# Latent layers of a PEER transformer, reworked as one stage each, in blocks of 128 tokens

## The reference

```python
for i in range(DEPTH):                     # 2
    h  = modulate(rms_norm_2(x, norm1_gain[i]), sh1, sc1)
    hc = modulate(rms_norm_2(xc, norm1_gain[i]), csh1, csc1)
    q, k, v = project_qkv(h, w_qkv[i], ..., rope)      # 8 heads, 2 kv heads, head width 128
    qc, kc, vc = project_qkv(hc, w_qkv[i], ..., None)
    o = latent attention over context and latent keys  # i = 0: global; i = 1: a window and a sink
    x = x + g1 * (o @ w_o[i])
    if not last: xc = xc + cg1 * (context_attention(...) @ w_o[i])
    h2 = modulate(rms_norm_2(x, norm2_gain[i]), sh2, sc2)
    x = x + g2 * peer_ffn(h2, ...)
    if not last: xc = xc + cg2 * peer_ffn(h2c, ...)
```

## Time and profile before

| | us |
|---|---|
| runs | 3165.12, 3167.58, 3170.16 |
| median | 3167.58 |
| span of the profiled execution | 3163.4 |
| context's layer 0 (stages up to) | 284 |
| first block, layer 0 and layer 1 end at | 860 and 1428 |
| latent layer 0: attention, experts begin at | 1489, 1648 |
| latent layer 1: begins, attention, experts begin at | 2293, 2372, 2524 |
| `write_out` begins at | 3158.8 |
| busy: TensorE, VectorE, GpSimd, ScalarE | 2598.7, 2245.3, 1215.8, 584.7 |

### The profile page before, as it was taken

How to read it: one execution, slowest core, us unless ns; L and a number is a source line. 1 busy time by engine, 2 the same in 40 slices (tenths; PEclk the granted TensorE clock), 3 DMA queues, 4 the chain that set the end, 5 groups by cost and what they waited for, 6 DMA issues and landing times.

```text
span 3163.4 us, 30793 instructions
## 1 busy us (share of the span) xinstructions
PE 2598.7 (82%) x10048; PEld 1719.6 (54%) x10048; DVE 2245.3 (71%) x5446; ACT 584.7 (18%) x1613; POOL 1215.8 (38%) x1028
## 2 busy tenths in 40 slices
PE   6798786899797679998898787777799987877776
PEld 2677664788675568886683332332367733333222
DVE  0438978699788877768778886665563698866555
ACT  2221212100021120002321111121214211111111
POOL 0002543466564355651434444444200254444441
PEclk8899898999898899999999999999999999999999
DMA  9327876799998489994779999999731599999997
GB/s 391 148 95 250 323 277 226 274 386 390 374 347 317 170 303 380 409 409 163 240 263 420 420 420 420 420 420 420 314 109 54 232 419 420 420 420 420 420 420 290
DMA packets 209521, 1029.22 MB, mean 325 GB/s; under 512 B 23409, under 2 KB 24945, under 8 KB 142929
## 3 DMA queue, kind: packets, MB, share of 16 engines
q0 software_dynamic: 147456, 805.37, 63.9%
q1 hardware_dynamic: 60624, 217.34, 18.2%
q10 hardware_dynamic: 1280, 4.54, 0.4%
HBM read 1021.98 MB, written 5.18 MB: 325 GB/s over the span
## 4 chain that ended last, share of the span: by engine, by line
DMA 35%; PE 35%; DVE 22%; issue 4%; ACT 1%; POOL 1%; SPq 1%; DVEq 0%; ACTq 0%; another core or an unknown queue 0%; POOLq 0%
DMA w_ring<-in_peer_uv,expert 11%; PE ps L2410 6%; DMA own<-in_peer_uv,expert 6%; DMA ctx_ring<-in_peer_uv,expert 5%; PE ps L2060 5%; DVE sum L1442 4%; PE ps L449 4%; PE ps L1172 4%; PE ps L1253 3%; DMA w_ring<-in_weights 3%; PE ps L1759 3%; DMA ctx_ring<-in_peer_v,ctx_expert 3%; DMA hT<-in_peer_uv,expert 2%; DMA low<-in_peer_uv,expert 2%; DVE ctx_ring L1445 1%
## 5 line engine op out<-in xcount | busy, mean ns | idle before, releaser
L2410 PE MATMUL ps<-w_ring,diag 128*128 128x512 f32 x876 | 425.6, 631 | 120.6 <-ACT diag L2355 120.6
L2410 PEld LDWEIGHTS ps<-w_ring,diag 128*128 128x128 f32 x876 | 167.2, 199 | 374.6 <-ACT diag L2355 194.6
L2197 DVE SCALAR_TENSOR_TENSOR w_ring<-w_ring,htok 128x1024 f32<-128x1024 f32 x219 | 267.7, 1223 | 138.9 <-DMA w_ring<-in_peer_uv,expert 137.7
L2249 POOL DMA_INDIRECT w_ring<-in_peer_uv,expert x219 | 240.7, 1099 | 312.7 <-PE ps L2410 269.2
L1253 PE MATMUL ps<-mix,w_ring 128*128 128x256 f32 x1408 | 307.5, 382 | 8.8 <-DVE mix L395 8.8
L1425 POOL DMA_INDIRECT ctx_ring<-in_peer_u,ctx_expert x126 | 160.1, 1270 | 399.3 <-DVEq L1992 247.8
L1253 PEld LDWEIGHTS ps<-mix,w_ring 128*128 128x128 f32 x1408 | 269.6, 192 | 46.7 <-issue 9.6
L2355 ACT ACTIVATE diag<-consts_sb 128x128 f32<-128x128 f32 x512 | 179.0, 394 | 614.2 <-DVE consts_sb L2290 592.8
L1425 POOL DMA_INDIRECT ctx_ring<-in_peer_v,ctx_expert x152 | 187.8, 1235 | 230.2 <-DVE sum L1442 144.8
L2249 POOL DMA_INDIRECT own<-in_peer_uv,expert x75 | 83.8, 1117 | 346.2 <-DVEq L1992 260.9
L2410 PE MATMUL ps<-ctx_ring,diag 128*128 128x512 f32 x296 | 142.8, 618 | 41.2 <-ACT diag L2355 41.2
(11 more groups left out here) (437 smaller groups left out, 5027.6 us busy)
## 6 DMA issues: line engine op xcount, KB each, us to landing
w_ring<-in_weights SPq DMA_DIRECT2D x392, 512.0 KB
w_ring<-in_peer_uv,expert POOLq DMA_INDIRECT x219, 24.4
ctx_ring<-in_peer_v,ctx_expert POOLq DMA_INDIRECT x152
ctx_ring<-in_peer_u,ctx_expert POOLq DMA_INDIRECT x126
ctx_more<-in_peer_v,ctx_expert POOLq DMA_INDIRECT x104
consts_sb<-in_consts SPq DMA_DIRECT2D x1, 1536.0 KB, 9.8
ctx_more<-in_peer_u,ctx_expert POOLq DMA_INDIRECT x80
own<-in_peer_uv,expert POOLq DMA_INDIRECT x75
```

What stands on the lines that cost most here:

```text
L2197: v.scalar_tensor_tensor(out=u, in0=u, scalar=1.0, in1=m.htok[:, e // SLOTS, :], op0=ALU.mult, op1=ALU.mult, accum_out=m.dots[:, e:e + 1]) ...
L2249: pool.indirect_dma_start(out=entry(e), out_offset=None, in_=table, in_offset=bass.IndirectOffsetOnAxis(ap=m.expert[:, blk, k:k + 1], axis ...
L2410: ins = pe.matmul(m.ps[:, 2 * blk + half, :], b.diag[:, e % DIAGS, :], entry(e)[:, D + half * 512:D + (half + 1) * 512], start=(k == 0), s ...
```

## The change

Each latent layer becomes one stage (`latent_layer`), and its work goes by blocks of 128 tokens with tokens on the partitions:

- Products have 128 tokens as the stationary operand and 512 columns of weights as the moving one. An item is the keys and values of a block, or 4 heads' queries of a block. Layer 0 makes 6 items before attention; layer 1 makes 3, since its context's keys and block 0's keys and queries are made at the end of layer 0. Head norms are squares by ScalarE summed along the row, a root and a reciprocal a few elements wide. The gains of the heads are multiplied into the rotation's tables (`make_tables`).
- The stream stays by token (`m.x`). Its gates are needed as rows, so the gates of a layer are written to DRAM (`keep_gates`, in the context's projection and in the middle of layer 0) and read back to all partitions.
- The order is: attention of block 0, its output product, norm, queries of its first pair, routing steps 0 to 3; then attention of block 1 with steps 4 to 7 behind its first four heads. GpSimd starts the gathers there. Everything else stands between entries (`beside(e)` on TensorE, ScalarE and VectorE): the output product of block 1, the queries of the 7 other pairs of both blocks and their routings, in the order `SEQUENCE`, and in layer 0 the context's stream and the next layer's first items.
- Entry places: in layer 0, 4 own, 2 of the context's ring and the old stream's, 7 in all, and an eighth from entry 120; in layer 1 these 8 from the start, 2 more from entry 12 and 6 of the weight ring from entries 72, 88 and 104. A place taken again waits for `s.used` of its last entry.
- In layer 0 the weight groups of `peer_w_q` 1 to 3 and of the next layer's first items are loaded while entries run.
- The shares of the context rows change: in the first layer 30, 50, 24, 16, 106 (before 30, 48, 22, 16, 110), in the second 36, 50, 21, 17, 127 (before 114 in the last, `feed_forward`), in latent layer 0 35 (before 48). In that layer 3 rows stand behind each item and 2 behind each head of block 0.
- The output is written by token and in parts at the end of layer 1; the stage `write_out` is gone.

`project_qkv`, `second_attention` and `peer_queries` remain for the context alone, as `project_context`, `context_attention` and `context_queries`; `peer_experts` and `Entries` are gone.

```diff
-STAGE_SEMS = 46
+STAGE_SEMS = 56
...
-WEIGH_AT = (3, 1)
+WEIGH_AT = (2, 1)
...
-                    rows.take(v, 4 if j < WEIGH_AT[l] else 3 + j % 2, "feed_forward")
+                    rows.take(v, 4, "feed_forward")
...
-    FIRST_SHARE = dict(in_projection=30, rwkv=48, attention=22, out_projection=16, feed_forward=110)
-    SECOND_SHARE = dict(in_projection=36, rwkv=50, attention=21, out_projection=17, feed_forward=114)
-    TAIL_SHARE = dict(project_qkv=8, attention=16, out_projection=14, peer_queries=10)
+    FIRST_SHARE = dict(in_projection=30, rwkv=50, attention=24, out_projection=16, feed_forward=106)
+    SECOND_SHARE = dict(in_projection=36, rwkv=50, attention=21, out_projection=17, feed_forward=127)
+    TAIL_SHARE = dict(latent=35)
...
+def keep_gates(sp, m, i, kept):
+
+    for n, part in enumerate((G1, G2)):
+        sp.dma_start(m.kept_gates[i, n].rearrange("(k p) -> p k", p=P), m.mods[:, i, part:part + KT, LATENTS],
+                     allow_slow_non_contiguous=True).then_inc(kept, 16)
+    sp.wait_ge(kept, 32)
...
+SEQUENCE = ((0, 0), (0, 1), (0, 2), (1, 0), (0, 3), (1, 1), (1, 2), (1, 3))
+QUERY_AT = {1: 4, 2: 14, 3: 28, 4: 42, 5: 58, 6: 74, 7: 90}
+ROUTE_AT = {1: (14, 1), 2: (24, 2), 3: (44, 2), 4: (64, 2), 5: (84, 3), 6: (111, 3), 7: (145, 3)}
+X1_AT = 3
+MODS_AT, SUMS_AT, CONTEXT_AT = 106, 108, 116
+HTOK_AT = 124
+X0_AT = 130
+NEXT_AT = 140
...
+        opened = {f"own{j}": (0, None) for j in range(OWN)}
+        if i:
+            opened.update(ring0=(0, None), ring1=(0, None), stream=(0, None), sums=(0, None),
+                          keys=(12, (s.o_done, 2 * PAIRS)), queries=(12, wide.filled(("out", 1, 1))))
+            for j in range(1, NG_PQ):
+                slot = ring.slot_of[g0 + G_PQ + j]
+                for half in range(2):
+                    opened[f"group{2 * slot + half}"] = (QUERY_AT[PLACE_OF[1, j]] + 14, wide.filled(("pq", 1, j)))
+        else:
+            opened.update(ring0=(0, (m.ctx_used, TT * 2 * SLOTS)), ring1=(0, (m.ctx_used, TT * 2 * SLOTS)),
+                          stream=(0, turned.filled(("x", 1, 1))),
+                          sums=(SUMS_AT + 12, turned.filled(("sums", KT // 2 - 1))))
...
         @block.gpsimd
         def _(pool):
+            pool.wait_ge(m.joined, JOINING * m.stages)
             for e in range(TOTAL):
                 blk, k = e // SLOTS, e % SLOTS
                 if k % PAIR_SLOTS == 0:
-                    pool.wait_ge(m.routed, routed_count(1 + i, blk, k // PAIR_SLOTS))
...
+                    pool.wait_ge(m.routed, len(SEQUENCE) * (1 + i) + PLACE_OF[blk, k // PAIR_SLOTS] + 1)
+                if entries.before[e]:
+                    sem, count = entries.before[e]
+                    pool.wait_ge(s.used if sem is None else sem, count)
                 pool.indirect_dma_start(out=entry(e), out_offset=None, in_=table,
...
+            attend(0, None if i else lambda h: rows.take(v, 2, "latent"))
...
+            for half in range(2):
+                add_out(0, half)
+            norm_rows(("h2", 0))
+            norm_first_half(("h2", 0))
+            for at in range(4):
+                route_step(0, at)
+
+            def first_route(h):
+                if h < 4:
+                    route_step(0, 4 + h)
+                if h == 4:
+                    routes[0].shift(0, PAIR)
+            attend(1, first_route)
...
+                for n, (start, every) in ROUTE_AT.items():
+                    at = e - start
+                    if at >= 0 and at % every == 0 and at // every < Route.STEPS:
+                        route_step(n, at // every)
...
+                for n, at in QUERY_AT.items():
+                    if at <= e < at + 4:
...
+                        query_part(n, 2 * (e - at), 2 * (e - at) + 2)
```

More of the change, by code:

```diff
@@ L1522, in final_gain @@
     return m.vectors[:, FINAL_AT + k:FINAL_AT + k + 1]
-def write_out(nc, m, d):
-    with stage(m, "written") as (block, s, b):
-        @block.sync
-        def _(sp):
-            sp.dma_start(d.out, m.xT[:, :, :]).then_inc(s.written, 16)
-            sp.wait_ge(s.written, 16)
 def build(nc, d):
@@ new lines @@
+ENTRY_PLACES = [f"own{j}" for j in range(OWN)] + ["ring0", "ring1", "stream", "sums", "keys", "queries"] + [
+    f"group{j}" for j in range(2 * WSLOTS)]
+SEQUENCE = ((0, 0), (0, 1), (0, 2), (1, 0), (0, 3), (1, 1), (1, 2), (1, 3))
+PLACE_OF = {bg: n for n, bg in enumerate(SEQUENCE)}
+QUERY_AT = {1: 4, 2: 14, 3: 28, 4: 42, 5: 58, 6: 74, 7: 90}
+ROUTE_AT = {1: (14, 1), 2: (24, 2), 3: (44, 2), 4: (64, 2), 5: (84, 3), 6: (111, 3), 7: (145, 3)}
+X1_AT = 3
+MODS_AT, SUMS_AT, CONTEXT_AT = 106, 108, 116
@@ new lines, with __init__ @@
+class EntryPlaces:
+    def __init__(self, m, i, opened):
+        self.m = m
+        last = {}
+        self.place, self.before, self.turn = [], [], []
+        for e in range(TT * SLOTS):
+            free = [name for name in opened if opened[name][0] <= e]
+            name = min(free, key=lambda name: (last.get(name, opened[name][0] - 8), ENTRY_PLACES.index(name)))
+            self.place.append(name)
+            self.before.append((None, last[name] + 1) if name in last else opened[name][1])
+            last[name] = e
+            m.entries_landed[name] += 16
+            self.turn.append(m.entries_landed[name])
+    def of(self, e):
+        m, name = self.m, self.place[e]
+        if name.startswith("own"):
+            return m.own[:, int(name[3:]), :]
+        if name.startswith("ring"):
+            j = int(name[4:])
+            return m.ctx_ring[:, 2 * j:2 * j + 2, :].rearrange("p s n -> p (s n)")
+        if name == "stream":
+            return m.xT[:, :, :].rearrange("p k t -> p (k t)")
+        if name == "sums":
+            return m.low[:, 3 * D:5 * D]
+        if name == "keys":
+            return m.low[:, D:3 * D]
+        if name == "queries":
+            return m.qT[:, :, :].rearrange("p k t -> p (k t)")
+        j = int(name[5:])
+        return m.w[:, j // 2, 2 * D * (j % 2):2 * D * (j % 2 + 1)]
+    def landed(self, e):
+        return self.m.entry_in[self.place[e]], self.turn[e]
@@ new lines, in _ @@
+            for n in range(len(made)):
+                item_rows(n)
+                if not i:
+                    rows.take(v, 3, "latent")
+            attend(0, None if i else lambda h: rows.take(v, 2, "latent"))
+            if not i:
+                rows.take_rest(v, "latent")
+            for half in range(2):
+                add_out(0, half)
[8 more added lines that the diff above has]
+                    routes[0].shift(0, PAIR)
@@ L2315, in _ @@
             for e in range(TOTAL):
-                if between and e == CONTEXT_AT + 2:
-                    context_back()
-                if e >= EARLY_DOTS:
-                    entry_dot(v, m, entries, e, s.dotted)
+                dot(e)
                 n = e // BATCH
@@ L2423, in context_first @@
+                beside(e)
+            weigh(TOTAL // BATCH - 1)
+            if between:
+                v.wait_ge(s.used, TOTAL)
+            else:
+                v.wait_ge(s.used, TOTAL)
+                for half in range(2):
+                    add_rows(("end", 1), half, m.ps[:, 2 + half, :])
 def context_first(nc, m, d, ring):
```

1123 lines of the change are left out of this document (765 added, 358 removed).

## The result

The changed kernel takes 3189.88 us (median of 4 runs, 3188.21 to 3195.68) against 3168.87 us before: **ratio 1.0073, 95% interval 1.0053 to 1.0093**, slower by 0.7%. 3098 was forecast, with a range to 3155. The profiled execution has a span of 3193.9 us (TensorE's mean granted clock 0.931, before 0.945). It is the slowest of the four (3195.68), and the profiled one of before was the fastest of its four (3165.12): the two traces are 30.5 us apart, the medians 21.0. So a difference of a few us between two traces is not by itself the edit's.

A forecast was written before the change was run, and what follows sets the result against it. Entry transfers were taken to bound the latent layers, with DMA mostly free before the first gathers; 3163.4 + 5 + 0 + 14 - 16 - 73 = 3093.4, with 4.2 around it 3098 us, range 3055 to 3155.

The forecast's parts named there:

- (a): Layer 0, entries 0 to 9 with output and query products on TensorE: 12 us lost by entry 14.
- +14: Second layer's feed_forward: 13 more rows are 16.7 us of transfer, partly hidden by slipping weight prefetch; bounds 0 and 25.
- that cancels, 0: First layer: feed_forward has 4 rows fewer, two earlier stages 2 more each, at 1.28 us a row; bounds -5 and +5.
- with three context rows (3.5 us) behind each: Layer 0 before attention: six items at 2.1 or 2.9 us, each followed by three rows, 37 us in all.
- (c): Layer 0's other entries, a step every second or third entry and six products of 4 entries: 6 us lost.
- hold of 14.3 us: How long an entry's place is held: 9.1 us from dot to reusing gather plus 5.2 from issue to landing.
- (b): Layer 0, entries 14 to 21, a whole routing at one step an entry: 4 us lost.
- 255 x 2.49 = 635: Transfer time from first to last entry landing in a latent layer, at 2.49 us an entry.
- B: Places short in layer 0: 2.86 us an entry up to 120, 44 us lost, 3120 to 3150 us; chance 0.14.
- C: Slower than before: places held some 20 us or more in layer 0; 3259 us at 24 us; chance 0.10.
- D: Slower serial chain to the first gather, 15 to 20 us a layer, 3130 us; chance 0.10.
- E: Better: the 13 rows slip under the next stage, weights hide the first entries' stretch, 3060 us; chance 0.08.

The follow-up runs named there:

- shares_back: Changed kernel with context rows moved back, 114 in the second layer's feed_forward and 48 in latent layer 0: 3176.01 us, ratio 1.0024.
- late_items: Changed kernel with squares, rows, turning and copies of the next layer's items made 2 to 4 entries later in layer 0: 3171.58 us, ratio 1.0013.
- no_loop_gates: `late_items` plus `shares_back` and 8 more context-row places, without the gate write in layer 0's loop (layer 1 uses layer 0's gates): 3144.47 us, ratio 0.9933.
- late_norm: `late_items` plus `shares_back`, with block 1's output product added 2 entries later and block 0's sum and norm steps later: 3156.69 us, ratio 0.9983.
- spread: `late_items` plus `shares_back` and 8 more context-row places, with query products from the fourth on in one-entry steps: 3137.81 us, ratio 0.9915.
- places3: Changed kernel with 3 own entry buffers instead of 4: 3234.03 us, ratio 1.0211.
- best: `late_items`, `shares_back`, 8 more context-row places and `late_norm`'s steps, with layer 0's gates written in the context's attention stage: 3136.83 us, ratio 0.9916.

## Why the prediction was wrong

**What held.** The idle time before the gathers is what the change recovers: layer 1, where it has places enough, gained 51 us (870.0 to 818.6; forecast 73). The bytes in layer 0's loop were right (14.4 MB for 14.3, 34 us at 0.42 MB/us), and the first stretch, (a), came out as summed: 22 lost with its two weight groups against 21.6 measured. The gates cost 6.8 for 5, within the bounds of 1 and 12, though the load of constants was no cover beside which they ran but a queue in which they waited.

**Feed-forward, second layer, +14 taken, +28 measured.** The term was mis-sized, and the 28 lie outside its bounds of 0 and 25. The bytes were right (16.7 us). But the sum let the next weights' prefetch slip against them, and the rows behind TensorE's last large product had nothing beside them but that prefetch: TensorE stood idle 29.5 us there for 2.2 before, and over the stage the DMA rate was 384 GB/s for 399. `shares_back` took back 25 of the 28. On the first layer "that cancels, 0" was wrong too: the stage got 7.7 us shorter with 4 rows fewer, while rwkv grew by 2.2. No run took that apart, and the point at which the rows are weighed had moved there as well.

**The first gather of layer 0, 143 taken, 168 measured.** The largest failed step is "with three context rows (3.5 us) behind each": it priced a row at VectorE's time, as if it had landed. Set beside the sum, the timeline of the changed kernel gives where the 25 us came up (from the layer's begin):

| | forecast | measured |
|---|---|---|
| norm, tables and x end | 14.4 | 14.4 |
| items and their rows end | 53 | 67.0 |
| attention of block 0 | 86 | 106.3 |
| output product | 100 | 120.4 |
| query product begins | 108 | 129.5 |
| scores | 119 | 142.2 |
| routing steps 0 to 3 | 128 | 151.5 |
| first gather | 143 | 168.1 |

Of the 14 us that the items lost, 9.2 are VectorE's waits for rows and 4.8 its waits for the items' roots. In all it waited 11.2 us for rows in this stretch. The rest is spread: a head of block 0 took 4.3 us and not 4.0, the norm of block 0 9.1 for 7.7, and the query's products 8.86 us for 6.9, at a granted clock of 0.80 after a stretch in which TensorE was busy 2 of 9 us. More places take the waits for rows away: with 48 rows, 12 places for 4 brought the first gather from 179.5 to 164.6 us, and the waits from 19.6 us to none. That the 143 of the sum agrees with the 143.6 without rows is chance: the sum had 39 us of rows in it (21 behind the items, 19 behind the heads, less 1.4) and left out the waits for TensorE's products and for the roots that appear when the rows are gone.

**The entries of layer 0, 22 lost by the forecast beyond the transfers, 68 measured (737 - 635 - 34).** This is outside the bounds of 5 and 60. The failed step is (c), "about 1 each: 6", and behind it the hold of 14.3 us, taken from a kernel whose engines ran in step. The step counted how busy each engine is over 16 entries, and not in what order the three meet. From an entry's dot to the gather that reuses its place the sum had 9.1 us; in the changed kernel it took 10.3 us on average for entries 16 to 120 and 11.6 for 144 to 208, and again 8.8 for 208 to 240, where no work is left between entries. Shown by a run: 17.5 us are the five waits for the next items' roots (`late_items`). Of the loss in entries 112 to 128, 5 us are the scattered write (`no_loop_gates`), though about half of them comes back behind it. Stretch (b) lost 9.2 for 4. The rest, some 18 us spread over entries 32 to 144, no run took apart; `late_norm` and `spread` show that two plain causes carry at most a small part of it, and that the loss grows by 30 with one place fewer (`places3`) ties it to the places.

**The transfers, 255 x 2.49 = 635.** This term left out what the kernel before itself loses: from first to last landing it took 653.5 us in layer 0 and, with no weights in the loop, 648.1 in layer 1. In layer 1 the changed kernel took 672.3 for a forecast of 655. Of these 17 us, 13 are thus in the kernel before too. Its first gather came 7 us late (129.2 for 122, at a granted clock of 0.86), which no run took apart.

**Which rival.** Rivals B and C named the mechanism of layer 0's entries, places held too long, and C the direction of the whole; their hold was too simple. B's 44 lost was under the measured 68, C's 183 far over. D, a slower chain to the first gather, happened as well: 25 us in layer 0 and 7 in layer 1 for the 15 to 20 it gave each, in layer 0 more by waits for rows than by D's lower clock. E's slip under the next stage did not happen. No rival alone gives the result: errors of one sign, 14 us in feed_forward, 25 and 46 in layer 0 and 22 in layer 1, added up. Three of them lay outside what the sum had allowed: 28 for at most 25, 68 for at most 60, and 168 for a first gather that was to be wrong over 165. So the single bounds were too narrow, and the range, which ended at 3155, treated them as if they could not come together: with all the upper limits at once (12, 5, 25 and 60, and the first gathers at 165 and 140) the sum would have been 3199.

**Two prices that a page spoke to.** Packets under 512 bytes rose from 23409 to 27696 in the profile's count of packets. 4096 of these 4287 are the four writes' elements, and so the Trainium skill's rule (DMA: Bandwidth & Descriptors, Rules for kernel authors) that a non-contiguous last dimension becomes one descriptor per element agrees. The estimate of 1.3 us with the page's figure per packet shares it out over 16 engines, which is the prediction's own step and not the page's; it came out near what the elements themselves took (nearly all in 1.3 us in the changed kernel and 1.7 in `best`). The fixed part near 2 us does not agree: the landing came 6.2 us after the last element, and 7.7 in `best`. On its rule about the ports (SBUF — State Buffer, Who interferes with whom), some of the gathers issued beside VectorE's operations on 128 x 1024 took 1.92 to 1.94 us in the changed kernel too (1480.14, 1487.00, 1496.25), others there 0.94 to 1.5, and with VectorE idle never over 1.0, which agrees in part; no run here took that second away, so what it costs the whole stays open.

## What to carry to other kernels

When work is laid between the steps of a streaming loop, each engine's place in the loop counts: an engine that runs ahead must not ask, at step n, for what an engine 3 steps behind makes at step n - 2; leave more steps between than the distance of the engines. Where gathered rows are used one behind the other, a row costs its round trip divided by its places if that is more than the operation that uses it (3.1 us for 1.28 here), and rows that stand where the engine waits anyway cost less than either (0.44 to 0.85 each in the runs here); look for buffers that are empty in that stretch. Before work is moved into or out of a stage, find the knee at which the stage changes from one engine's floor to another's, here TensorE's 243 us at 114 rows.

## What the runs showed of the hardware

- A write of scattered 4-byte elements landed long after its last element had gone out: 2048 elements in two writes landed 6.2 us (changed kernel) and 7.7 us (`best`) after it. From the issue of the second write it was 15.70 us behind a load of weights and constants (DMA share 1.03), and 11.2 us with two small stores beside it.
- A DMA share near 1 went with 406 GB/s (0.98, layer 0's entries before), 383 GB/s (0.98, the changed kernel) and 356 GB/s (0.95, 2080 to 2200 us, without weights): the share alone does not tell whether gathers were always queued.
- Between a tanh and a root ScalarE loaded a function table for 1.28 us, and again on the way back; one such load lies in the wait of 5.45 us above.
